# Mirrored order of the pairs of query blocks in both attention stages of a two-layer decoder

## The reference

```python
# layer A, 16 heads; the selection enters as a mask over all causal keys
logits = q . k + rel_bias[t5_bucket(t - s)]       # masked where not selected
p = softmax(logits);  o = p @ v

# layer B, 8 heads, two maps of width 64 each, values of width 128
logits = q . k + rel_bias[t5_bucket(t - s)]       # masked where s > t
p = softmax(logits).reshape(heads, 2, block, L)
a = p[:, 0] - lam * p[:, 1]
o = a @ v
```

## Time and profile before

| | us |
|---|---|
| median of three runs (lowest to highest) | 3811.56 (3802.57 to 3811.91) |
| profiled execution | 3815.45 |
| its span, first to last instruction | 3813.8 |
| attention A, 16 heads, 874 to 1742 | 868 |
| attention B, 8 heads, 2760 to 3532, and the end of its last outputs | about 780 |

### The profile page before, as it was taken

The page is one execution under the profiler, slowest core; times in us unless marked ns, Lnnn a source line. Parts: engine busy times, 40 slices in busy tenths (PEclk is TensorE's granted clock), DMA queues, the critical chain, the costliest instruction groups (busy, mean ns, idle before and its releaser), DMA issues. The chain is left out here.

```text
span 3813.8 us, 65226 instructions
## 1 busy us (share of the span) xinstructions
PE 3443.9 (90%) x18786; PEld 2572.1 (67%) x18786; DVE 2136.0 (56%) x5870; ACT 2016.5 (53%) x3490; POOL 523.0 (14%) x550
## 2 busy tenths in 40 slices
PE   5879898888999999998977999999888888889799
PEld 3756454476666666666856888889866666666687
DVE  3669999995555555655644111000087777777344
ACT  2558899946777777774223111111166666666222
POOL 2000355001111111110220111121020000000011
PEclk8989999978999999998988999999999999999889
DMA  8661789563222232224542444222232222221442
GB/s 237 181 148 26 220 238 238 167 229 94 80 75 83 82 80 75 81 76 169 174 142 89 117 122 122 77 77 67 76 111 66 70 67 70 70 67 34 142 139 100
DMA packets 430046, 436.41 MB, mean 114 GB/s; under 512 B 81792, under 2 KB 341280, under 8 KB 429600
## 3 DMA queue, kind: packets, MB, share of 16 engines
q1 hardware_dynamic: 417984, 429.65, 38.3%
q10 hardware_dynamic: 11872, 4.46, 1.0%
HBM read 271.44 MB, written 162.53 MB: 114 GB/s over the span
## 5 line engine op out<-in xcount | busy, mean ns | idle before, releaser
L1387 DVE CUSTOM_DVE_ANT_0 a_att_sb_lg<-a_att_ps_s,mask 128x512 f32<-128x512 f32 (+3 forms) x512 | 302.5, 596 | 217.3 <-PE a_att_ps_s L1279 176.5
L1453 ACT ACTIVATE b_att_sb_lg<-b_att_sb_lg,b_att_sb_negm 128x384 f32<-128x384 f32 (+15 forms) x256 | 305.6, 1198 | 127.0 <-DVE b_att_sb_negm L1395 126.8
L1285 PE MATMUL b_att_ps_s<-b_att_sb_k,b_att_sb_q 64*128 64x512 f32 (+3 forms) x1920 | 294.8, 418 | 85.6 <-DVE b_att_sb_lg L1389 71.4
L1461 ACT ACTIVATE a_att_sb_pT<-a_att_ps_t 128x512 f32<-128x512 f32 (+3 forms) x640 | 316.0, 530 | 104.6 <-PE a_att_ps_t L1298 97.8
L1453 ACT ACTIVATE a_att_sb_lg<-a_att_sb_lg,a_att_sb_negm 128x384 f32<-128x384 f32 (+15 forms) x256 | 307.3, 1201 | 78.6 <-DVE a_att_sb_negm L1395 78.6
L1298 PE MATMUL a_att_ps_t<-ident,a_att_sb_lg 128*128 128x128 f32 x2176 | 340.0, 279 | 0.0
L1389 DVE TENSOR_SCALAR_CACHE_REDUCE b_att_sb_lg<-b_att_ps_s 128x512 f32<-128x512 f32 (+3 forms) x512 | 282.9, 590 | 98.5 <-PE b_att_ps_s L1285 78.1
L1815 DVE TENSOR_SCALAR_CACHE_REDUCE mask<-scores,threshold_bits 128x384 bf16<-128x384 f32 (+8 forms) x288 | 322.6, 1187 | 1.2
L1298 PEld LDWEIGHTS a_att_ps_t<-ident,a_att_sb_lg 128*128 128x128 f32 x2176 | 248.7, 141 | 107.4 <-issue 57.4
L1278 PE MATMUL a_att_ps_s<-a_att_sb_k,a_att_sb_q 128*128 128x512 f32 (+3 forms) x640 | 287.3, 449 | 26.5 <-DVE a_att_sb_mx L1387 15.9
L1315 PE MATMUL a_att_ps_o<-a_att_sb_pT,a_att_sb_v 128*64 128x256 f32 (+1 forms) x2304 | 297.4, 377 | 0.2 <-DMA a_att_sb_v<-scratch_v 0.2
(11 more groups left out here) (302 smaller groups left out, 7020.9 us busy)
## 6 DMA issues: line engine op xcount, KB each, us to landing
a_att_sb_q<-scratch_qT SPq DMA_DIRECT2D x512, 64.0 KB, 2.5
select_sb_w_gate<-in_a_w_in SPq DMA_DIRECT2D x32, 512.0 KB, 5.4
mask_sb_mod_w<-in_mod_w SPq DMA_DIRECT2D x16, 1024.0 KB, 6.8
a_att_sb_k<-scratch_kT SPq DMA_DIRECT2D x128, 128.0 KB, 2.8
b_att_sb_q<-scratch_qT SPq DMA_DIRECT2D x128, 128.0 KB, 2.5
b_att_sb_k<-scratch_kT SPq DMA_DIRECT2D x64, 256.0 KB, 4.2
b_qkgv_sb_w<-in_b_w_in SPq DMA_DIRECT2D x30, 512.0 KB, 4.7
front_sb_mod_w<-in_mod_w SPq DMA_DIRECT2D x8, 1024.0 KB, 7.8
```

The costliest lines, as they stand in the source:

```text
L1285: mm = nc.tensor.matmul(s_ps[:, (n + m) % SR, 0:z - a], q[rows, p // 2 % QS, x, cols], k[rows, slot, y, a:z], start=(j == 0), stop=(j == 2))
L1387: x = nc.vector.tensor_tensor_reduce(out, src, tab, 1.0, 2 * NEG, sign, ALU.max, top[:, col:col + 1])
L1453: nc.scalar.activation(buf, buf, ACT.Exp, bias=negm[:, p, m:m + 1], accum_out=sums[:, b, ds(h * M + m, 1)]).then_inc(exp_done, 1)
L1461: nc.scalar.activation(pT[:, r % 2, a:z, c:c + P], t_ps[:, n % TR, 0:z - a], ACT.Copy).then_inc(t_left, 1)
```

## The change

One table is written in another order:

```diff
-PAIRS = [1, 3, 5, 7, 6, 4, 2, 0]
+PAIRS = [0, 2, 4, 6, 7, 5, 3, 1]
 ORDER = [2 * r + i for r in PAIRS for i in range(2)]
 NCH = [len(chunks(b)) for b in ORDER]
```

## The result

| | us |
|---|---|
| after, median of ten runs (lowest to highest) | 3822.57 (3816.09 to 3825.23) |
| before, ten runs beside it | 3811.33 (3802.57 to 3815.54) |
| ratio, with its 95% interval | 1.0026 (1.0018 to 1.0034) |
| profiled execution after (span, clock) | 3822.19 (3820.6, 0.945) |

The account below looks back on a forecast made before the run. PE was taken to bound A, DVE and PE each half of a head in B. Terms +1 (B), 0 (place 6 starts), +6 (A) on 3815.45 gave 3822 profiled, about 3818 on the median's scale; range 3792 to 3838.

Parts of the forecast that it names:

- instead of 6: Attention A, 16 heads: added PE waits in the rising half, +0.4 us a head, +6 us in all, bounds -16 to +24.
- was to lose 1: Attention B, 8 heads: waits nearly unchanged, +1 us in all; start and end effects of some 3 us each cancel.
- The failed step: A, places 6 and 7: PE mostly sets the pace itself, so waits hardly grow; +0.4 us a head.
- My rival: A, places 4 to 9: ACT's chain sets the pace, PE's waits grow 0.7 to 1.5 us a head; 3831 us, chance 0.30.
- The signal for it: A: PE's weight loads waiting on DVE before L1278, forecast 50 to 65 us; clearly over 3.5 a head favours the rival.
- the DVE account: B: DVE's pieces and mixes set the steps where it comes last; seven new steps of 4.5 to 7.7, sum 43.5 us.
- DVE comes last at places 4 to 10: B, new order: exponentials wait on the maximum at places 4 to 10 instead of 2 to 9.
- I took +0.1: B, each head: DVE's lead over PE stays 8.3 us; +0.1 us a head taken, +1 for 8 heads.
- -1.0 as a bound: B, each head: setting each place's mix against PE's work of its own place favours the new order by 1.0 us.
- the starts of place 6: B, loop body start: seven "issue" stalls of 3.6 to 3.9 us stay, slow clock behind them costs the same; 0 us.
- the rule cited in the prediction: A taken branch to a target outside the two pages an engine holds forces a fetch before it goes on.
- some 3 us less: B's first head begins with blocks 0 and 1 instead of 2 and 3: some 3 us less before DVE's place 4.

Follow-up runs that it names:

- the runs of B alone: New order in attention B only, old order in A, against the kernel before: 3809.29 us, ratio 0.999.
- the late output: DVE's output half in A moved behind the next place's first chunk, loop body one place later: 3827.16 us with new order in A, 3814.74 with old order.
- four places: A given four accumulator places for chunks and two for transposes, instead of two and four: 3820.08 us with new order in A, 3838.73 with old order.
- the middle alone: A takes the new order only in its middle (pairs 1, 3, 4, 6, 7, 5, 2, 0), B old, against the kernel before: 3830.77 us, 1.005.
- the cut of the short chunk: Blocks 4, 8, 12 end in chunks of three and two key blocks, not four and one: 3821.18 us with new order in A, 3801.91 with old order.
- the best kernel here: Old order in A, new in B, last chunks of blocks 4, 8, 12 cut three and two in both, against the kernel before: 3786.01 us, 0.9935.
- the last kernel: The best kernel here, plus a wait delaying POOL's split of output weights in B until place 10 of the first head: 3785.80 us, 0.9931.

## Why the prediction came out as it did

**The total** was near by luck, because two misses of opposite sign cancel in part. A lost 12.7 instead of 6. B with its end was to lose 1 and gained some 4 (-4.3 in the runs of B alone, -3.6 by the profiles).

**A, direction right, size off by a factor of two, holder wrong.** The failed step is "PE measured within 0.2 of its need at places 6 and 7 ... so it is nearer the second, and I take +0.4 a head". That term was sized at 0.4 and measured 0.74. That PE was the bound there before says nothing once its work falls by 1.4 us in those two places: the pace of the engine next in line then shows, and waits went from 0.2 to 1.05. My rival's 0.7 to 1.5 a head contains the measured 0.74. But its mechanism, ACT's copy holding DVE, fell with the late output; what the runs leave is DVE's pace against two accumulator places (four places take the wait and the loss at places 6 and 7 away, the middle alone brings them). DVE's pace itself was not varied alone; the cut of the short chunk, which frees a place sooner, is the nearest to it. The signal for it was badly chosen, as the weight loads show above: they stayed at 55.1, inside the 50 to 65 of the forecast, while A lost twice what was forecast.

**B, the DVE account held for the steps.** The sum of 43.5 and the length of each step (within 0.3) came as forecast. "DVE comes last at places 4 to 10" did not: the waits are at places 2 to 9. The last head changed by -0.5 us from first to last maximum, where I took +0.1 and kept -1.0 as a bound.

**B, the starts of place 6.** Taken as 0, measured about -2 us in the six heads that have them (places 6 and 7 cost 5.4 beyond their work against 5.7). That is no more than chance: with the old order in B, the kernel with the new order in A alone has 5.2 (19.8 against 14.5). The stall was neither lost nor multiplied, but there are six and not seven. In the two traces a stall lasts 2.9 to 3.9 us. By the rule cited in the prediction, of the Trainium skill ("Runtime: NRT & Kernel Launch", section "Instruction fetch mechanics"), they could belong to the branch back to the body's start; the trace agrees in their place and in their absence from the first head. A's loops show no stall of over 0.3 us, and no run here tests the rule.

**B, the first head.** I let "some 3 us less" at the start cancel against 3 more behind the end, and both came: from the start of the first head to its maximum of place 4 it is 14.1 us instead of 16.7, that is 2.5 less, and the end cost 3.1. The other 3.0 of the first head's 5.5 come from something that I had not read: POOL splits the next stage's weights there. DVE and POOL in the kernel before, first head of B:

```profile
2791.00 4.03 DVE L1407 SCALAR_TENSOR_TENSOR b_att_sb_lg<-b_att_sb_lg,b_att_sb_ratio 128x1536 f32<-128x1536 f32 x1
2791.03 2.37 POOL L1256 TENSOR_TENSOR b_out_w_lo<-b_att_sb_out_raw,b_out_w_hi 128x1024 fp32r<-128x1024 f32 x1
...
2802.93 4.43 DVE L1407 SCALAR_TENSOR_TENSOR b_att_sb_lg<-b_att_sb_lg,b_att_sb_ratio 128x1920 f32<-128x1920 f32 x1
2802.96 2.39 POOL L1256 TENSOR_TENSOR b_out_w_lo<-b_att_sb_out_raw,b_out_w_hi 128x1024 fp32r<-128x1024 f32 x1
```

The two mixes last 2.2 us longer than the 1.82 and 2.22 that these widths take in the next heads. The steps of places 7 and 8 were 12.05 and 11.33 us, against 7.76 and 7.05 in the third head. After the change:

```profile
2801.38 1.55 DVE L1407 SCALAR_TENSOR_TENSOR b_att_sb_lg<-b_att_sb_lg,b_att_sb_ratio 128x1280 f32<-128x1280 f32 x1
2801.54 2.29 POOL L1254 CAST b_out_w_hi<-b_att_sb_out_raw 128x1024 fp32r<-128x1024 f32 x1 [98.01 <-DMA b_att_sb_out_raw<-in_b_w_out]
...
2816.14 2.36 POOL L1256 TENSOR_TENSOR b_out_w_lo<-b_att_sb_out_raw,b_out_w_hi 128x1024 fp32r<-128x1024 f32 x1
...
2816.89 1.63 DVE L1405 SCALAR_TENSOR_TENSOR b_att_sb_ratio<-sums,b_att_sb_rec,neglam 128x1 f32<-128x1 f32 x1
```

Now the mixes keep their time and POOL's cast waits (2.29 instead of 1.04); what DVE loses, it loses in an instruction of one column, 1.63 instead of 0.22. Places 8 and 9 still take 9.36 and 9.31 us, against 7.62 and 7.89 in the third head, a loss of 3.2; places 7 and 8 lost 8.6 before. This is how the two executions met and not what the order does: with the new order in B alone a mix of 4.16 us is back and the first head takes 94.2, while the seven other kernels with the old order and the old chunks in B have 93.2 to 94.7.

## What to carry to other kernels

Reordering work that only changes which sizes meet should be priced at each place by the engine next in line: where the bound engine loses work, its lead over the second is the most that is gained, and what goes beyond it comes back as waits. Test such a change stage by stage: the same table gained in one stage and lost in the other, and the best kernel here, 0.65% faster, has it in one only. Compare a stage over several executions before explaining a few us of it: one pair showed 10.9 us in B with 4.5 lost behind it, where eleven runs of B alone showed a gain of 4.3 in all. The value of a cut depends on the order in which it runs (in B nothing in one order and 1.2 us a head in the other), so it has to be measured there.

## What the runs showed of the hardware

POOL and DVE ran one after the other where they met, and the one that had to wait carried the other's time in its own duration. With POOL's work put at another time, in the last kernel:

```profile
2801.64 1.04 POOL L1263 CAST b_out_w_hi<-b_att_sb_out_raw 128x1024 fp32r<-128x1024 f32 x1 [121.98 <-DVE b_att_sb_mx L1396]
2802.73 4.55 DVE L1416 SCALAR_TENSOR_TENSOR b_att_sb_lg<-b_att_sb_lg,b_att_sb_ratio 128x2048 f32<-128x2048 f32 x1
2802.76 2.37 POOL L1265 TENSOR_TENSOR b_out_w_lo<-b_att_sb_out_raw,b_out_w_hi 128x1024 fp32r<-128x1024 f32 x1
2805.07 3.10 POOL L1263 CAST b_out_w_hi<-b_att_sb_out_raw 128x1024 fp32r<-128x1024 f32 x1
```

4.55 is 2.35 of its own and 2.2 of POOL's; the cast behind is 3.10 instead of 1.04. DVE's copies out of the accumulator kept their 0.69 us beside POOL; only instructions with two operands in SBUF grew, even one of a single column. The Trainium skill ("SBUF — State Buffer", section "SBUF: two separate sides") says that DVE's instructions with two SBUF inputs and POOL's share a pair of ports under an exclusive lock, held for a whole instruction. The trace agrees, and such a lock shows in no wait of the profile, only in a duration that is too long for its width. The recorded starts don't tell who had to wait: the mix of 4.55 us stands 0.03 ahead of POOL's instruction.
